# A two-block transformer stack on one core: mask matmul of the causal attention on the diagonal keys alone

## What is computed

```
# mixer (once in each of 2 layers): 8 heads, query/key width 64 + 32 = 96
def attend(qn, qp, blk):                    # one block of 128 queries, 2 blocks
    sc = (qn . k_nope + qp . k_pe) * scale  # 128 x 256 scores for each head
    mask = key_idx[None, :] <= q_idx[:, None]
    sc = where(mask, sc, finfo.min)
    return softmax(sc) @ v
# fox (once): 16 heads, width 64, and two rows for the bias
    s = q . k * scale + ci[..., None] - ck[:, :, None, :]
    s = where(key_pos[None, :] <= qpos[:, None], s, -1e30)
    p = softmax(s);  o = p @ v
```

## Time and profile before

| what | value |
|---|---|
| median of 3 runs | 2114.37 us |
| profiled execution, its own time | 2112.89 us |
| its span, first to last instruction | 2111.1 us |
| mean granted TensorE clock | 0.985 |
| TensorE busy | 96% of the span |

### The profile page before, as it was taken

One profiled execution on the slowest core, in us unless ns is written; L12 is line 12 of the kernel. 1 busy time (PEld: TensorE's weight loads), 2 busy tenths in 40 slices (PEclk: granted clock), 3 DMA queues, 4 the chain that ended last, 5 costly groups with the idle time before them and its releaser, 6 DMA issues.

```text
span 2111.1 us, 26411 instructions
## 1 busy us (share of the span) xinstructions
PE 2035.4 (96%) x9851; PEld 1678.6 (80%) x9866; DVE 1238.3 (59%) x1366; ACT 1011.2 (48%) x1279; POOL 240.9 (11%) x357
## 2 busy tenths in 40 slices
PE   8999988999999999988999999999999999999998
PEld 6888867778888888867778887778778888888887
DVE  5555579865545555669865545555556455446554
ACT  5445664544445445664445444544445434455433
POOL 1000168000000000069000002111100000000000
PEclk9999998999999999999999999999999999999999
DMA  7554442545555555542455554444335554425552
GB/s 266 189 189 176 175 151 89 175 159 202 196 181 184 204 179 186 184 150 87 155 182 201 187 183 158 144 141 152 140 109 190 188 190 160 162 78 182 206 180 100
DMA packets 54626, 354.16 MB, mean 168 GB/s; under 512 B 7696, under 2 KB 8336, under 8 KB 12816
## 3 DMA queue, kind: packets, MB, share of 16 engines
q1 hardware_dynamic: 53968, 352.51, 47.1%
q10 hardware_dynamic: 576, 0.53, 0.1%
HBM read 351.97 MB, written 1.05 MB: 167 GB/s over the span
## 4 chain that ended last, share of the span: by engine, by line
PE 83%; DVE 7%; ACT 4%; DVEq 2%; issue 2%; POOL 1%; DMA 1%; POOLq 1%; SPq 0%; ACTq 0%
PE psum L1809 58%; PE psum L1860 17%; DVE wlo L1022 3%; DVE arena L1243 2%; ACT whi L557 2%; PE psum L1875 1%; DVEq L1237 1%; PE psum L1938 1%; PE psum L2230 1%; PE psum L2251 1%; DMA raw<-w_stream 1%; PE psum L2237 1%; PE psum L1821 1%; PE psum L2015 1%; POOL arena L1651 1%
## 5 line engine op out<-in xcount | busy, mean ns | idle before, releaser
L1022 DVE TENSOR_TENSOR wlo<-raw,whi 128x2048 fp32r<-128x2048 f32 x325 | 745.0, 2294 | 447.9 <-ACT whi L557 447.8
L1809 PE MATMUL psum<-whi,xTh 128*128 128x512 f32 (+1 forms) x1936 | 769.0, 397 | 14.8 <-DVE xTl L1048 5.2
L1809 PE MATMUL psum<-whi,xTl 128*128 128x512 f32 (+1 forms) x1936 | 752.9, 389 | 0.0
L1809 PE MATMUL psum<-wlo,xTh 128*128 128x512 f32 (+1 forms) x1936 | 752.8, 389 | 0.0
L557 ACT ACTIVATE whi<-raw 128x2048 fp32r<-128x2048 f32 x325 | 621.1, 1916 | 258.1 <-PE psum L1860 151.3
L1809 PEld LDWEIGHTS psum<-whi,xTh 128*128 128x128 f32 x1936 | 366.9, 190 | 93.2 <-issue 5.9
L1809 PEld LDWEIGHTS psum<-whi,xTl 128*128 128x128 f32 x1936 | 366.8, 189 | 76.3
L1809 PEld LDWEIGHTS psum<-wlo,xTh 128*128 128x128 f32 x1936 | 367.5, 190 | 69.4
L1860 PE MATMUL psum<-whi,braT 128*128 128x512 f32 x1056 | 337.7, 390 | 0.0
L1860 PEld LDWEIGHTS psum<-whi,braT 128*128 128x128 f32 x1056 | 198.3, 188 | 41.1
L1860 PE MATMUL psum<-wlo,braT 128*128 128x512 f32 x528 | 205.5, 389 | 0.0
(11 more groups left out here) (236 smaller groups left out, 1449.2 us busy)
## 6 DMA issues: line engine op xcount, KB each, us to landing
raw<-w_stream SPq DMA_DIRECT2D x326, 1024.0 KB, 4.8
bias<-chunks SPq DMA_DIRECT2D x18, 256.0 KB, 5.0
x<-x_in SPq DMA_DIRECT2D x2, 512.0 KB, 5.1
raw<-w_stream SPq DMA_DIRECT2D x4, 256.0 KB, 7.3
arena<-gate_w SPq DMA_DIRECT2D x2, 512.0 KB, 5.1
arena<-fins SPq DMA_DIRECT2D x2, 512.0 KB, 5.8
con<-consts SPq DMA_DIRECT2D x1, 720.0 KB, 10.9
out<-x ACTq DMA_DIRECT2D x2, 256.0 KB, 2.3
```

The source lines that it names most:

```text
L1022: TT(wlo[:, r], raw[:, r], whi[:, r].bitcast(F32), ALU.subtract).then_inc(lo_done, 1)
L1809: ins = pe.matmul(dst(rb), s(kt)[:, rows], w[:, r, at_:at_ + cols], start=start and n == 0 and k == 0, stop=stop and n == len(kts) - 1 and ...
```

## The change

In `qk`, `rb` = 0 stays as it is: one mask matmul and one product of 128 columns. For `rb` = 1 the mask matmul covers the own (diagonal) 128 keys alone, with the mask that `rb` = 0 uses; the product for these keys follows in the same accumulation; then the product for keys 0 to 127 runs as an accumulation of its own, without a mask, with the same q as weights. The signal moves to that last matmul. The loop over groups goes (there is one group everywhere).

```
-                    keys, dst = (rb + 1) * P, scores(groups, h, rb)
-                    per = max(1, min(groups, W // keys))
-                    for g0 in range(0, groups, per):
-                        gs = range(g0, min(g0 + per, groups))
-
-                        cols = slice(g0 * keys, (gs[-1] + 1) * keys)
-                        pe.matmul(dst[:, cols], identb[:], masks[rb][:, cols], start=True, stop=False)
-                        for g in gs:
-                            ins = pe.matmul(dst[:, g * keys:(g + 1) * keys], q_of(h, g)[:, rb * P:(rb + 1) * P],
-                                            k_of(h, g)[:, 0:keys], start=False, stop=g == gs[-1])
+                    dst, own, q = scores(groups, h, rb), slice(rb * P, (rb + 1) * P), q_of(h, 0)[:, rb * P:(rb + 1) * P]
+                    pe.matmul(dst[:, own], identb[:], masks[0], start=True, stop=False)
+                    ins = pe.matmul(dst[:, own], q, k_of(h, 0)[:, own], start=False, stop=True)
+                    for before in range(rb):
+                        keys = slice(before * P, (before + 1) * P)
+                        ins = pe.matmul(dst[:, keys], q, k_of(h, 0)[:, keys], start=True, stop=True)
                     signal(ins, s_in, groups, rb)
```

## The result

The changed kernel took 2120.30 us (median of 10 runs, 2117.46 to 2121.97) against 2114.43 us before (10 runs, 2111.75 to 2115.95): 5.9 us more, ratio 1.0028, 95% interval 1.0019 to 1.0038. The forecast was 2114.5 us, within 0.2%, with a range that ended at 2117.2. Its profiled execution took 2120.13 us, with a span of 2118.3 us and a mean granted clock of 0.976, where it was 0.985.

The account below looks back on a forecast made before the run. TensorE, busy 96% of the span, was taken to bound the kernel, except the mixers' attentions (VectorE). Fox's 14 heads at 0.01 us gave +0.14, mixers nothing: 2114.5 us against the median 2114.37, range 2112.4 to 2117.2.

Parts of the forecast that it names:

- Fox: Fox's attention, bound by TensorE: second block 0.56 us against 0.55, 0.01 us more for each of 14 heads, +0.14 us.
- second product at 0.28: Rival, second block: the added 128-column product costs 0.28 us like the first, not 0.22; +1.0 us, 2115.4; chance 0.18.
- loads laid bare: Rival, second block: both added weight loads stand uncovered, 0.31 us more a head, +4.3 us, 2118.7; chance 0.03.
- stream alone: Rival, second block: weight loads stay hidden, so the mask's half is saved; -0.8 us, 2113.6; chance 0.13.
- The mixers: nothing: Both mixers' attentions, bound by VectorE: scores are ready before VectorE takes them, so the change adds nothing.
- slack of 0.89 us: Mixers, head 5: scores end at 336.67 and VectorE takes them at 337.56; the shortest slack found.
- signs: Wrong if: second product under 0.20 or over 0.30 us, mixers' row maximum waiting for a product, more lower-clock windows with TensorE full.
- The clock rival: In either mixer, changed activity adds or removes a lower-clock stretch of 1.3 us: 2115.8 or 2113.2; no separate chance for one.
- Slower by four stretches: Mixers: four lower-clock stretches of one sign, upward, about 2119.7 us; chance 0.03, shared with unknown fetching costs.

Follow-up runs that it names:

- Fox alone: The change in fox's attention only, mixers as in the kernel before: 2114.23 us against 2113.51 for the kernel before, ratio 1.0003.
- mixers alone: The change in the two mixers' attentions only, fox as in the kernel before: 2121.48 us against 2113.51 for the kernel before, ratio 1.0034.
- split alone: Kernel before with the second block's product in two 128-column matmuls, mask still 256 wide, everywhere: 2113.45 us against 2113.51, ratio 0.9999.
- Mask twice: Changed kernel with the second block's 128-column mask matmul issued twice, everywhere: 2120.33 us against 2113.51 for the kernel before, ratio 1.0032.

## Why the prediction was wrong, step by step

*Fox.* Right in mechanism and size. The second block is 0.06 + 0.28 + 0.22 us; the mask's half isn't saved, which fits the forecast's reason, that its stream covered a weight load. The 0.11 us a step, which the forecast read as the load, is these products' stream as well (256 columns take 0.43 us in two instructions); the row that sets a load apart is pv's, 0.39 us for four matmuls of 64 columns, 0.10 us each. Fox alone measured +0.7 us, with an interval that holds the forecast +0.14 and zero, so the size is read from the chain and not from the time. The rivals "second product at 0.28" and "loads laid bare" are out by the 0.22 in the chain, "stream alone" by the whole second block, 0.56 us where it needed 0.49.

*The mixers: nothing.* This is the step that failed: the change was put at nothing there, and the mixers alone measured a ratio of 1.0034. It compared the added time, at most 0.14 us a head, with a slack of 0.89 us, and took the clock's course as given. That slack was read at head 5, whose scores ended as the full level had just come back. In the changed kernel head 5's row maxima wait 1.24 us. The statement that the scores are ready before VectorE turns to them holds for a full clock; at the lower level a round of 3.41 us is longer than VectorE's 2.0 to 2.6 us, and the kernel before was spared only because the stretch was short. The added time was not what mattered: it is about nil at the lower level too (3.41 in both). Two of the signs that the prediction had named for being wrong came: row maxima of the mixers that wait for a product, and more windows at the lower clock where TensorE is full. TensorE's own waits hardly showed it: for the exponentials they are 5.6 and 5.4 us, near the forecast 5.5 and 6.5.

*The clock rival.* It named the place, and left the direction open. Its price was twice too high: 1.3 us for 4.0 us at the lower level is 0.33 for each. The mean clock of 0.976 for 0.985 makes some 38 us more at that level (an estimate, 2 x 0.009 x 2118), so 12 us by this price, and the mixers lost 6.35 us in the profile. Slower by four stretches was given 0.03, together with unknown costs of fetching, because the change in TensorE's work is a few hundredths of a us a head, and because it took several stretches to be separate events. They are not separate. What TensorE does in a round at the lower level decides whether the full level returns (split alone against the changed kernel, and the changed kernel against the same with 512 columns more a round), and the round repeats for each head, so where it doesn't return it mostly stays away for all heads that are left. What I listed in favour, that the work between the waits is "not quite the same", was the cause.

*Shown and not shown.* Shown: the loss is in the mixers; the falling clock is its cause, since matmuls that keep the clock up take the loss away; the split alone doesn't bring it, and it comes where the split product has the narrow mask; and one or two matmuls of 512 columns put into each round end it. Not shown: that the narrow mask in its old place brings the loss without the split, and what exactly makes the level return, the number of columns or the length of a matmul. Mask twice went either way, and one of the ten runs of the changed kernel had a clock of 0.981 and took 2117.46 us, which suggests that these kernels stand near an edge.

The Trainium skill, "TensorE: Matmul & The Clock Gate", section "Why this matters for your kernels", advises to keep TensorE continuously busy to reach the full clock, and to avoid idle gaps. For the fall at 326 us the trace agrees: it comes after a wait of 2.6 to 2.7 us, and with the waits filled it is gone. For the return the trace differs: TensorE is busy 10.00 of 10.00 us at 0.50, and 11.00 of 11.00 at 0.51, by the profile's busy time. The measurement decides here: TensorE, busy and loading weights for 9.88 of 10.00 us, stayed at the lower level.

## What to carry to other kernels

Before trimming what TensorE streams in a part where its clock is at the lower level, compare the length of a round at that level with the round of the engine that bounds the part. Where TensorE's is longer (3.41 us against 2.0 to 2.6 here), the clock decides the time, and the slack read at the full level is no cover. Where a matmul's stream covers the next weight load, making it narrower need not shorten anything: the second block took 0.56 us where it took 0.55. Where TensorE waits ahead of a run of small matmuls, a few matmuls that nobody reads are a cheap insurance (here the changed kernel's ratio went from 1.0028 to 0.9995), though not a gain in itself where another engine bounds the part.

## What the runs showed of the hardware that was not expected

- TensorE stayed at the lower level through 21 us without a gap that the profile shows (10.00 of 10.00 us busy at 0.50, then 11.00 of 11.00 at 0.51), in rounds of 128-column float32 matmuls, 64-column ones and transposes.
- More work made it faster: 512 columns more a round, a ratio of 1.0008 where the changed kernel had 1.0028.
- Two bf16 matmuls of 128 columns did not stand in for one of 256: 3.52 us a round at the lower level, against 3.41 in the kernel before, and 2120.33 us where split alone, with the one wide matmul, took 2113.45.
